# A transformer stack on one core: the working buffers laid out at multiples of 128 bytes

## The reference

```python
for l in range(2):                       # first block
    x = x + 0.5 * rms_norm(swiglu(rms_norm(x, nw[0]), gate, up, down), nw[1])   # F = 2816
    m = even_mixer(...) if l % 2 == 0 else odd_mixer(...)   # attention + pooling / conv + state-space scan
    x = x + rms_norm(m, nw[3])
    x = x + 0.5 * rms_norm(swiglu(rms_norm(x, nw[4]), gate, up, down), nw[5])
for l in range(2):                       # second block
    x = x + rmsnorm(token_mixer(rmsnorm(x, pre_mix_g), ...), post_mix_g)        # two attentions, gated
    f = jnp.square(jax.nn.relu(rmsnorm(x, pre_ffn_g) @ w_ffn_up)) @ w_ffn_down  # F2 = 4096
    x = x + rmsnorm(f, post_ffn_g)
```

## The kernel before

| starts before | buffers |
|---|---|
| 0 | x, xh, xl, w_lo, w_hi, ident, y |
| 96 | sqsum (116576), tmp, work (122720), hh (139104), hl, hh2, hl2; even mixer from e_pw to m_hi, m_lo |
| 64 | second block: 139104 + 9216 (b_tab) + 96 (b_small) = 148416, and so c_hi, ya_hi, b_turned, b_va, b_vb, yb_hi, mm_hi and their partners |
| 32 | odd mixer from o_x (147104) on, z_hi, g_hi among them |

## Time and profile before

### The profile page before, as it was taken

How to read it: one execution, slowest core, us unless ns; L and a number is a source line. 1 busy time by engine, 2 the same in 40 slices (tenths; PEclk the granted TensorE clock), 3 DMA queues, 4 the chain that set the end, 5 groups by cost and what they waited for, 6 DMA issues and landing times.

```text
span 3564.7 us, 45985 instructions
## 1 busy us (share of the span) xinstructions
PE 3524.4 (99%) x18316; PEld 2860.5 (80%) x18316; DVE 1429.9 (40%) x2294; ACT 1351.8 (38%) x2200; POOL 1953.1 (55%) x2418
## 2 busy tenths in 40 slices
PE   9999999999999999999999999999999999999999
PEld 8888868888888888748888886788888877888887
DVE  4221666221522148776322267325111475244022
ACT  4332354232323235674332337334233345334231
POOL 6555545555565548744655457555555465546553
PEclk9999999999999999999999999999999999999999
DMA  4333302333233332203333320132333210323332
GB/s 137 95 92 97 100 19 96 99 94 94 92 100 95 92 95 95 69 1 98 95 100 92 100 80 18 60 96 89 95 99 96 94 52 13 95 83 101 95 95 77
DMA packets 87717, 301.53 MB, mean 85 GB/s; under 512 B 9936, under 2 KB 14544, under 8 KB 87120
## 3 DMA queue, kind: packets, MB, share of 16 engines
q1 hardware_dynamic: 85392, 296.50, 26.8%
q10 hardware_dynamic: 2112, 2.10, 0.2%
HBM read 296.46 MB, written 2.10 MB: 84 GB/s over the span
## 4 chain that ended last, share of the span: by engine, by line
PE 54%; DVE 3%; ACT 1%; issue 0%; DMA 0%; ACTq 0%; DVEq 0%
PE bank L317 13%; PE bank L319 13%; PE bank L318 13%; PE bank L880 2%; PE bank L857 2%; PE scores L842 1%; PE bank L1951 1%; PE bank L1953 1%; PE bank L1952 1%; DVE sqsum L518 1%; PE bank L1333 1%; PE bank L1335 1%; PE bank L1369 1%; DVE xl L508 1%; DVE tmp L439 1%; DVE x L446 1%
## 5 line engine op out<-in xcount | busy, mean ns | idle before, releaser
L306 POOL TENSOR_TENSOR w_lo<-w_raw,w_hi 128x256 fp32r<-128x256 f32 x2210 | 1682.0, 795 | 1412.8 <-ACT w_hi L284 1398.0
L284 ACT ACTIVATE w_hi<-w_raw 128x1024 fp32r<-128x1024 f32 (+2 forms) x565 | 584.5, 1037 | 1214.5 <-DMA w_raw<-in_ffn_up 374.2
L317 PE MATMUL bank<-xh,w_hi 128*128 128x512 f32 x2544 | 998.8, 393 | 2.3 <-DVE o_g L1596 1.2
L319 PE MATMUL bank<-xh,w_lo 128*128 128x512 f32 x2544 | 990.2, 389 | 0.0
L318 PE MATMUL bank<-xl,w_hi 128*128 128x512 f32 x2544 | 990.0, 389 | 0.0
L317 PEld LDWEIGHTS bank<-xh,w_hi 128*128 128x128 f32 x2544 | 478.3, 188 | 105.7 <-issue 3.1
L319 PEld LDWEIGHTS bank<-xh,w_lo 128*128 128x128 f32 x2544 | 478.4, 188 | 100.1
L318 PEld LDWEIGHTS bank<-xl,w_hi 128*128 128x128 f32 x2544 | 478.7, 188 | 99.6 <-issue 2.4
L317 PE MATMUL bank<-hh,w_hi 128*128 128x512 f32 (+1 forms) x1336 | 501.9, 376 | 0.0
L318 PE MATMUL bank<-hl,w_hi 128*128 128x512 f32 (+1 forms) x1336 | 500.9, 375 | 0.0
L319 PE MATMUL bank<-hh,w_lo 128*128 128x512 f32 (+1 forms) x1336 | 500.8, 375 | 0.0
(11 more groups left out here) (403 smaller groups left out, 4198.4 us busy)
## 6 DMA issues: line engine op xcount, KB each, us to landing
w_raw<-in_ffn_up SPq DMA_DIRECT2D x176, 512.0 KB, 3.5
w_raw<-in_ffn_down SPq DMA_DIRECT2D x64, 512.0 KB, 3.5
w_raw<-in_b_ffn_up SPq DMA_DIRECT2D x64, 512.0 KB, 3.5
w_raw<-in_b_ffn_down SPq DMA_DIRECT2D x64, 512.0 KB, 3.5
w_raw<-in_b_gates SPq DMA_DIRECT2D x48, 512.0 KB, 3.5
w_raw<-in_od_in SPq DMA_DIRECT2D x33, 512.0 KB, 3.3
w_raw<-in_ffn_down SPq DMA_DIRECT2D x32, 384.0 KB, 3.1
w_raw<-in_b_in SPq DMA_DIRECT2D x24, 512.0 KB, 3.4
```

What stands on the lines that cost most here:

```text
L284: act.activation(w_hi[:, g % RING, 0:widths[g]], w_raw[:, g % RING, 0:widths[g]], ACT.Copy)\
L306: ins = pool.tensor_tensor(w_lo[:, slot, part], w_raw[:, slot, part], w_hi[:, slot, part].bitcast(F32), ALU.subtract)
L317: pe.matmul(out, wh, hi, start=first, stop=False)
L319: return pe.matmul(out, wl, hi, start=False, stop=last)
```

## The change

Sizes and the order of buffers change; no instruction is added, taken away or moved. meancol grows to 14 floats (64 bytes), by which sqsum (116608 = 911 x 128), tmp, work (122752 = 959 x 128), hh (139136 = 1087 x 128) and hl start at 0 modulo 128. In the second block b_small grows from 96 to 1024 bytes, so that the buffers from c_hi on (149376 = 1167 x 128) do too. In the odd mixer, o_pick goes ahead and grows to 192 bytes and o_a takes 96, which puts o_x at 147328 = 1151 x 128. In the even mixer e_small and e_nsink take 64 bytes each and e_ident 512, and the padded e_u and e_a (4224 bytes each) go behind m_lo; e_pw then starts at 151552 = 1184 x 128. The instructions address the same elements as before in the larger buffers. x, y, xh, xl, w_hi, w_lo and ident stay where they were.

```diff
+SMALL2 = 256
-        meancol = sb("meancol", [P, 6])
+        meancol = sb("meancol", [P, 14])
-        e_tab, e_wg, e_small, e_nsink, e_mask, e_ident, e_pw, e_u, e_a, e_qk, e_v, m_hi, m_lo = over(
-            "hh", ("e_tab", [P, 2560], F32), ("e_wg", [P, 2, P], F32), ("e_small", [P, 14], F32),
-            ("e_nsink", [P, 6, 2], F32), ("e_mask", [P, 2, P], BF16), ("e_ident", [P, P], BF16),
-            ("e_pw", [P, 2, S], F32), ("e_u", [P, 2, S + 16], F32),
-            ("e_a", [P, 2, S + 16], F32), ("e_qk", [P, 8, S], F32), ("e_v", [P, 2, S], F32),
-            ("m_hi", [P, KD, S], F32R), ("m_lo", [P, KD, S], F32R))
-        odd_fixed = [("o_tab", [P, 2 + 2 * P], F32), ("o_small", [P, 234], F32), ("o_a", [32, 2], F32),
+        e_tab, e_wg, e_small, e_nsink, e_mask, e_ident, e_pw, e_qk, e_v, m_hi, m_lo, e_u, e_a = over(
+            "hh", ("e_tab", [P, 2560], F32), ("e_wg", [P, 2, P], F32), ("e_small", [P, 16], F32),
+            ("e_nsink", [P, 8, 2], F32), ("e_mask", [P, 2, P], BF16), ("e_ident", [P, 2 * P], BF16),
+            ("e_pw", [P, 2, S], F32), ("e_qk", [P, 8, S], F32), ("e_v", [P, 2, S], F32),
+            ("m_hi", [P, KD, S], F32R), ("m_lo", [P, KD, S], F32R), ("e_u", [P, 2, S + 16], F32),
+            ("e_a", [P, 2, S + 16], F32))
+        odd_fixed = [("o_tab", [P, 2 + 2 * P], F32), ("o_small", [P, 240], F32), ("o_a", [32, 24], F32),
+                     ("o_pick", [96, 96], BF16),
...
-                     ("o_pick", [96, 32], BF16), ("o_x", [P, KD, S], F32), ("o_b", [P, SG, S], F32),
+                     ("o_x", [P, KD, S], F32), ("o_b", [P, SG, S], F32),
...
-        tab2 = [("b_tab", [P, 4 * S + 2 * P], F32), ("b_small", [P, 24], F32)]
+        tab2 = [("b_tab", [P, 4 * S + 2 * P], F32), ("b_small", [P, SMALL2], F32)]
...
-        hi_b = over("hh", ("b_gap", [P, 4 * S + 2 * P + 24], F32), ("b_gap2", [P, 2 * (QR + KR) * S], F32),
+        hi_b = over("hh", ("b_gap", [P, 4 * S + 2 * P + SMALL2], F32), ("b_gap2", [P, 2 * (QR + KR) * S], F32),
...
-                sp.dma_start(e_small[:], t["ev_small"]).then_inc(tables_loaded, 16)
+                sp.dma_start(e_small[:, 0:14], t["ev_small"]).then_inc(tables_loaded, 16)
```

More of the change, by code:

```diff
@@ L165, in build @@
         BF16 = mybir.dt.bfloat16
-        e_tab, e_wg, e_small, e_nsink, e_mask, e_ident, e_pw, e_u, e_a, e_qk, e_v, m_hi, m_lo = over(
-            "hh", ("e_tab", [P, 2560], F32), ("e_wg", [P, 2, P], F32), ("e_small", [P, 14], F32),
-            ("e_nsink", [P, 6, 2], F32), ("e_mask", [P, 2, P], BF16), ("e_ident", [P, P], BF16),
-            ("e_pw", [P, 2, S], F32), ("e_u", [P, 2, S + 16], F32),
-            ("e_a", [P, 2, S + 16], F32), ("e_qk", [P, 8, S], F32), ("e_v", [P, 2, S], F32),
-            ("m_hi", [P, KD, S], F32R), ("m_lo", [P, KD, S], F32R))
-        odd_fixed = [("o_tab", [P, 2 + 2 * P], F32), ("o_small", [P, 234], F32), ("o_a", [32, 2], F32),
+        e_tab, e_wg, e_small, e_nsink, e_mask, e_ident, e_pw, e_qk, e_v, m_hi, m_lo, e_u, e_a = over(
[6 more added lines that the diff above has]
+                     ("o_pick", [96, 96], BF16),
                      ("o_r", [32, S], F32), ("o_dt", [P, 4, 32], F32), ("o_nr", [P, 4, 32], F32),
                      ("o_mask", [P, 2, P], BF16), ("identb", [P, P], BF16), ("o_r3", [96, S], BF16), ("o_part", [32, S], BF16),
-                     ("o_pick", [96, 32], BF16), ("o_x", [P, KD, S], F32), ("o_b", [P, SG, S], F32),
+                     ("o_x", [P, KD, S], F32), ("o_b", [P, SG, S], F32),
                      ("o_c", [P, SG, S], F32)]
-        o_tab, o_small, o_a, o_r, o_dt, o_nr, o_mask, identb, o_r3, o_part, o_pick, o_x, o_b, o_c, o_xt, o_z, o_g, o_cv = over(
+        o_tab, o_small, o_a, o_pick, o_r, o_dt, o_nr, o_mask, identb, o_r3, o_part, o_x, o_b, o_c, o_xt, o_z, o_g, o_cv = over(
             "hh", *odd_fixed, ("o_xt", [P, 4, D], F32), ("o_z", [P, KD, S], F32), ("o_g", [P, CONV_T, S], F32),
@@ L845, in attend_pe @@
                         for at, mask in u["masks"]:
-                            mm = pe.matmul(scores[g % 2][:, side, at:at + P], e_ident[:], e_mask[:, mask, :], start=False,
+                            mm = pe.matmul(scores[g % 2][:, side, at:at + P], e_ident[:, 0:P], e_mask[:, mask, :], start=False,
                                            stop=True, skip_group_check=True)
@@ L1087, in constants @@
             def constants():
-                ch.link(dve.tensor_scalar(e_nsink[:].rearrange("p j a -> p (j a)"), e_small[:, 2:14], -1.0, None, ALU.mult))
-                ch.link(dve.tensor_copy(e_ident[:], ident[:]))
+                ch.link(dve.tensor_scalar(e_nsink[:, 0:6, :].rearrange("p j a -> p (j a)"), e_small[:, 2:14], -1.0, None, ALU.mult))
+                ch.link(dve.tensor_copy(e_ident[:, 0:P], ident[:]))
                 ch.link(dve.tensor_copy(e_mask[:, 0, :], e_tab[:, 2 * S:2 * S + P]))
@@ L1184, in tables @@
                 sp.dma_start(o_tab[:], t["tab_odd"]).then_inc(odd_loaded, 16)
-                sp.dma_start(o_small[:], t["od_small"]).then_inc(odd_loaded, 16)
+                sp.dma_start(o_small[:, 0:234], t["od_small"]).then_inc(odd_loaded, 16)
             stream_sp(sp, c.blocks, t["od_in"], ODD_LINS, RING - 1, tables)
@@ L1530, in odd_dve @@
             for q in range(3):
-                ch.link(dve.tensor_copy(o_pick[32 * q:32 * (q + 1), :], ident[0:32, 0:32]))
+                ch.link(dve.tensor_copy(o_pick[32 * q:32 * (q + 1), 0:32], ident[0:32, 0:32]))
             taps = [(i, j) for j in TAPS for i in (0, 1)] + [(2, j) for j in TAPS]
@@ L1779, in tables @@
                 sp.dma_start(b_tab[:], t["tab_b"]).then_inc(tables_loaded, 16)
-                sp.dma_start(b_small[:], t["b_small"][i]).then_inc(tables_loaded, 16)
+                sp.dma_start(b_small[:, 0:24], t["b_small"][i]).then_inc(tables_loaded, 16)
             g = c.blocks
```

## The result

The changed kernel takes 3540.71 us (median of 5 runs, 3540.26 to 3542.59) against 3564.76, a ratio of 0.9929 with a 95% interval of 0.9918 to 0.994: 24.1 us less. The profiled execution spans 3538.9 us; its time was 3540.71, and in every run of the changed kernel the time lies 1.8 us above the span.

A forecast was written before the change was run, and what follows sets the result against it. TensorE, busy 3524.4 of 3564.7 us, was taken as the bound, its time the sum of matmul pitches. Terms -22.0 - 2.0 - 2.0 - 0.3 + 1.9 + 1.3 = -23.1 us gave 3542 us, range 3536 to 3552.

The forecast's parts named there:

- the pitch follows the start of the operands: All float32 matmuls of 512 columns: each operand's start modulo 128 sets the pitch; starts 0, 64, 96 give 226.6, 228.9, 233.3 ns.
- a pitch between 227 and 233: Sign in the profile after that the prediction is wrong; 226.6 ns was expected in the even mixer's output products.
- hh and hl: Feed-forward down-projections: 3288 matmuls of 512 columns go from 233.3 to 226.6 ns, 22.0 us less.
- From starts 96 and 32: Even and odd mixer products: 168 + 84 + 48 = 300 matmuls at 6.7 ns less each, 2.0 us less.
- From start 64: Output, branch and moving-c products: 876 matmuls, 2.0 us less; 48 with stationary c, 0.3 us less.
- Halves: 888 matmuls of 256 columns, on hh, mm, m and in the odd mixer: 2.1 ns dearer each, 1.9 us more.
- Transposes: 632 transposes, costed at the halves' 2.1 ns each: 1.3 us more, bounds 1.9 us either way.
- the other engines' nothing: ScalarE's copies, VectorE and GpSimd: alignment costed at no change, 0 us.
- half the gain: Rival: the operands' relation counts beyond 128 bytes, modulo 512, leaving hh at 228.9 ns; 3552.1 us, chance 0.07.
- Nothing changes: Rival: slow pitches belong to something else shared, such as the row's far end; 3564.7 us, chance 0.09.
- the line rule: Skill's SBUF rule: penalty per 16-byte line crossed; all buffers start on lines, so the same pitch, about 3565 us.
- Slower: Rival: 2784 short matmuls pay up to 3 ns in step while 512-column products gain nothing; 3573.1 us, chance 0.04.

## Why the prediction held, and which of its steps did not

The time was forecast at 3542 and measured at 3540.7, the saving at 23.1 and measured at 24.1 us. That the kernel is the sum of TensorE's pitches is borne out: waits stayed, and the 22 us came where the down-projections stand. One reading ahead of it was too coarse, that the granted clock is at 2.4 GHz throughout; it costs the forecast nothing, as both executions have five short stretches at 1.2.

The step that failed is the reading of the rows, "the pitch follows the start of the operands", each for itself modulo 128. What sets the pitch is the difference of the two starts modulo 256: the weights 640 bytes on lose everything and 42 us more than before without leaving a multiple of 128, and everything 96 bytes later loses nothing. The rows read before the change already held a hint: moving 64 over stationary 0 cost 228.9 ns and moving 0 over stationary 64 cost 232.9. I took it for a weight of the second operand of its own. It was the sign of a difference, 64 in one case and 192 in the other.

So the size of the gain is in part luck. The layout aimed at multiples of 128, and hh (1087 x 128), mm_hi and the odd mixer's operands happened to come to lie on odd multiples, like the weights (w_hi at 90240 = 705 x 128). On even multiples, where m_hi (from 1184 x 128 on) came to lie, hh would have the 232.7 ns of the run with the weights 640 bytes on. By that, an estimate, its 3288 products would have gained 2 us in place of 21.7. The prediction named a pitch between 227 and 233 as a sign of being wrong, and m_hi's 232.5 ns in place of 226.6 was that sign.

The terms, by the pitches of the two profiles:

- hh and hl: 22.0 forecast; 3288 x (233.3 - 226.7) = 21.7 us.
- From starts 96 and 32: 2.0 forecast, about 1.0 found. The odd mixer's 132 give it in full (233 to between 227 and 228 ns), the even mixer's 168 only 0.9 ns each, 0.2 us, because their difference went from 96 to 128 and not to 0. This is the mis-sized term, and the run with the even mixer in step shows that its cause is the one named.
- From start 64: 2.0 forecast; mm_hi 336 x 2.2 and ya, yb 384 x 2.8 (229.6 to 226.8) are 1.8. The 156 with moving c went from 229.8 to 229.3 only and the 48 with stationary c from 233.8 to 230, 0.3 us together. Those are short groups behind waits, and I haven't found why a difference of 0 does less there.
- Halves: 1.9 more forecast; 118.2 to 119.8 on 840 of them is 1.3 us, while the even mixer's 48 went from 119.6 to 118.5. The rows that spoke against the change were right, in this size.
- Transposes: 1.3 more forecast, nothing found, 1.09 us for eight as before. The extrapolation from the halves doesn't hold for 128 columns.

That is 21.7 + 1.0 + 1.8 + 0.3 - 1.3 = 23.5 us. The pitches come from the two profiled executions, whose spans differ by 25.8 us (3564.7 and 3538.9) and not by the medians' 24.1: the span of 3564.7 only happens to equal the median, since a time lies 1.8 us above its span, and the forecast took its 23.1 from there. Of the other 2.3 us, 1.0 is in xh's own products (227.2 to 227.0 ns on some 5000), 0.7 in the stretches at 1.2 GHz and 0.4 in matmuls behind waits. ScalarE's copy into hh takes 633 ns as before, and VectorE and GpSimd are busy 1430.6 and 1951.8 us where they were 1429.9 and 1953.1, so that the other engines' nothing holds too.

Of the rivals, "half the gain" had the better mechanism, that the relation of the operands counts beyond 128 bytes, with the wrong period and so the wrong time: xh against the weights differs by 0 and hh by 256 modulo 512, and both are at 227 ns. "Nothing changes" is out by hh's 226.7 ns. With it falls what the line rule of the Trainium skill would give here ("SBUF — State Buffer", section Specifications (TRN2)): all these starts lie on 16-byte lines, and the pitch still goes from 226.7 to 233.4 ns. "Slower" needs short matmuls that pay; they paid 1.6 ns at 256 columns and nothing at 128.

The Trainium skill's same page, section Who interferes with whom, gives TensorE two independent read ports, one for the moving operand and one for the weight load, and says that only the port pair shared by VectorE and GpSimd causes contention. No run here shows ports. What the runs show is that where the two operands lie against each other makes 6.7 ns of 227.

Shown by undoing and redoing: where the moving operands of a stream lie alike and both weight buffers do, the pitch depends on the difference modulo 256, at all eight multiples of 32, and not on where both lie. Shown by the lines of the two runs with one weight buffer moved: the weights of the next matmul count besides the own. Not shown: why. That the two reads hinder each other inside TensorE's path to the buffers fits all of this, and no run here looks there.

## What to carry to other kernels

When one engine is busy all the time, compare pitches of equal instructions between stages; a difference of 3% with nothing waiting was here a property of the operands, and it was worth as much as the instruction is frequent. Before reading a remainder as a rule, list every operand's full start and look at differences as well as at positions: one row at the same remainder with another price refutes the rule. An alignment that helps may do so only because it brings two buffers into step, so that a change of an unrelated small buffer between them can cost 2%: here 640 bytes moved ahead of the weights took 66 us.

## What was not expected of the hardware

- The pitch of a 512-column float32 product with its own weight load is 226.7, 228.9 or about 233 ns (232.7 to 234.3) by (moving - stationary start) modulo 256 of 0, 64 or any other multiple of 32, wherever in the partition's row both lie. That is so at the granted 2.4 GHz: in the stretches at 1.2 GHz it is 426.7 ns at differences of 0 and 192 alike.
- For 256 columns the order is another: 114.4 ns at 192, where 512 columns cost 233.3, and 119.8 at 0, where they cost 226.7. What is best for whole tiles is among the worst for halves.
- With w_hi and w_lo at different remainders modulo 256, the cheap pitch is left on one line of three at most: 3588.5 us with w_lo moved, 3613.9 with w_hi moved, against 3540.7.
